# First chunk of the memory keys and values: weights split on POOL into freed token places, turned keys copied earlier

## The reference, cut to what matters

```python
    mix = jnp.concatenate([a, r], axis=-1) @ w_out[l]
    x = x + rms_norm(mix, norm_mix_post[l])

    h = rms_norm(x, norm_xa_pre[l])
    mn = rms_norm(mem, norm_mem[l])
    q = (h @ xa_wq[l]).reshape(B, S, XA_HEADS, XA_HEAD_DIM)
    kv = (mn @ xa_wkv[l]).reshape(B, M, 2, XA_HEADS, XA_HEAD_DIM)
    s = jnp.einsum('bshd,bmhd->bhsm', q, kv[:, :, 0]).astype(jnp.float32) * (XA_HEAD_DIM ** -0.5)
    p = jax.nn.softmax(s, axis=-1).astype(x.dtype)
    xo = jnp.einsum('bhsm,bmhd->bshd', p, kv[:, :, 1]).reshape(B, S, D_MODEL) @ xa_wo[l]
    x = x + rms_norm(xo, norm_xa_post[l])
```

## Time and profile before

| | |
|---|---|
| median of 3 runs | 1456.83 us |
| the profiled execution | 1455.88 us, its span 1453.7 us |
| PE busy | 1413.0 us, 97% of the span |
| POOL busy | 815.1 us, 56% |
| DVE busy | 768.1 us, 53% |
| ACT busy | 610.3 us, 42% |
| granted TensorE clock | 0.999 of 2.4 GHz |
| chain that ended last | PE 82%, DVE 6%, POOL 4%, ACT 3%, DMA 3%, issue 2% |

### The profile page before, as it was taken

The page is one execution under the profiler, slowest core; times in us unless marked ns, Lnnn a source line. Parts: engine busy times, 40 slices in busy tenths (PEclk is TensorE's granted clock), DMA queues, the critical chain, the costliest instruction groups (busy, mean ns, idle before and its releaser), DMA issues.

```text
span 1453.7 us, 19794 instructions
## 1 busy us (share of the span) xinstructions
PE 1413.0 (97%) x7176; PEld 1193.0 (82%) x7176; DVE 768.1 (53%) x1185; ACT 610.3 (42%) x1259; POOL 815.1 (56%) x619
## 2 busy tenths in 40 slices
PE   7999999999999999999999999999999999999998
PEld 7999999766888777888788788888888888867886
DVE  5185048586983776757246843323333333353868
ACT  6111112666642655335446433333333333434454
POOL 1585455001864265530235687777777774699753
PEclk9999999999999999999999999999999999999999
DMA  5452112000025075320245333332333324933353
GB/s 220 149 172 74 50 45 66 0 1 1 9 61 222 34 253 156 94 74 0 85 168 186 104 99 104 109 102 98 106 109 109 107 75 155 366 95 94 99 209 150
DMA packets 119031, 160.29 MB, mean 110 GB/s; under 512 B 9120, under 2 KB 70816, under 8 KB 118944
## 3 DMA queue, kind: packets, MB, share of 16 engines
q1 hardware_dynamic: 115216, 148.93, 31.0%
q10 hardware_dynamic: 3728, 10.24, 2.0%
HBM read 122.17 MB, written 36.96 MB: 109 GB/s over the span
## 4 chain that ended last, share of the span: by engine, by line
PE 82%; DVE 6%; POOL 4%; ACT 3%; DMA 3%; issue 2%; SPq 0%; POOLq 0%; DVEq 0%; ACTq 0%
PE ps L1041 24%; PE ps L1043 24%; PE ps L1042 24%; PE ps L1037 4%; PE ps L1399 2%; DVE z L2541 1%; PE ps L1170 1%; PE ps L1264 1%; DMA raw<-in_xa_wkv_dram 1%; POOL wd L1010 1%; POOL w_lo L914 1%; PE ps L1198 1%; DMA gain_b<-f_rows 1%; PE ps L1242 1%; DVE sm L2416 1%
## 5 line engine op out<-in xcount | busy, mean ns | idle before, releaser
L1041 PE MATMUL ps<-w_hi,t_hi 128*128 128x352 f32 (+1 forms) x768 | 268.0, 349 | 3.7 <-POOL w_lo L930 2.6
L1043 PE MATMUL ps<-w_hi,t_lo 128*128 128x352 f32 (+1 forms) x768 | 265.9, 346 | 0.0
L1042 PE MATMUL ps<-w_lo,t_hi 128*128 128x352 f32 (+1 forms) x768 | 265.3, 345 | 0.0
L1041 PEld LDWEIGHTS ps<-w_hi,t_hi 128*128 128x128 f32 x768 | 144.7, 188 | 15.0 <-POOL w_lo L930 3.4
L1043 PEld LDWEIGHTS ps<-w_hi,t_lo 128*128 128x128 f32 x768 | 144.5, 188 | 11.0
L1042 PEld LDWEIGHTS ps<-w_lo,t_hi 128*128 128x128 f32 x768 | 144.7, 188 | 10.4
L819 POOL TENSOR_TENSOR w_hi<-raw,zero 128x352 fp32r<-128x352 f32 (+1 forms) x68 | 57.9, 852 | 110.7 <-PE ps L1043 110.3
L930 POOL TENSOR_TENSOR w_lo<-raw,w_hi 128x512 fp32r<-128x512 f32 x32 | 41.7, 1315 | 102.1 <-ACT w_hi L1978 101.9
L2864 DVE TENSOR_TENSOR ev<-ps,ev 128x512 f32<-128x512 f32 x21 | 14.5, 691 | 144.2 <-PE ps L1043 144.2
L1696 ACT ACTIVATE z<-ps 128x352 f32 x48 | 22.4, 466 | 162.0 <-PE ps L1043 161.5
L823 POOL TENSOR_TENSOR w_lo<-raw,w_hi 128x352 fp32r<-128x352 f32 (+1 forms) x68 | 77.0, 1133 | 5.3
(11 more groups left out here) (330 smaller groups left out, 3965.7 us busy)
## 6 DMA issues: line engine op xcount, KB each, us to landing
raw_a<-in_ffn_w_gu_dram SPq DMA_DIRECT2D x44, 256.0 KB, 3.1
raw_b<-in_ffn_w_gu_dram SPq DMA_DIRECT2D x44, 256.0 KB, 3.2
f_rows<-fs SPq DMA_DIRECT2D x44, 256.0 KB, 3.7
raw<-in_w_in_dram SPq DMA_DIRECT2D x60, 176.0 KB, 2.3
gain_b<-f_rows SPq DMA_DIRECT2D x39, 256.0 KB, 2.6
tables<-f_rows SPq DMA_DIRECT2D x38, 256.0 KB, 2.7
f_rows<-fa SPq DMA_DIRECT2D x33, 256.0 KB, 3.4
raw<-in_xa_wkv_dram SPq DMA_DIRECT2D x32, 256.0 KB, 3.6
```

The costliest lines, as they stand in the source:

```text
L1041: nc.tensor.matmul(out, a_hi, b_hi, start=start, stop=False, skip_group_check=onto)
L1042: nc.tensor.matmul(out, a_hi, b_lo, start=False, stop=False, skip_group_check=onto)
L1043: return nc.tensor.matmul(out, a_lo, b_hi, start=False, stop=stop, skip_group_check=onto)
```

## The change

The first product's eight units (c = 0) are handled in a new way. POOL waits until tiles 0 to 3 of the last output piece are done. From then on the columns 0 to 511 of `t_hi` and `t_lo` hold token features that nobody reads any more. POOL rounds each unit into `t_hi[:, k, 0:512]` and subtracts into `t_lo[:, k, 0:512]`, and PE reads the weights from there. ACT now rounds units 8 to 31 only, and DVE makes the low parts of units 10, 14, ..., 30 only. On ACT the four roundings ahead of the copy of output tile 7 stay, but they are those of units 8 to 11; the two groups of four behind it are gone. The last change is that the four copies to `kM` now stand ahead of the roundings of units 24 to 27.

The core of the diff:

```diff
@@ -132,7 +132,12 @@
 
 def kv_on_dve(n):
 
-    return n % RING == 2
+    return n >= NK and n % RING == 2
+
+
+def kv_lows(n):
+
+    return n // RING - 1
 
 
 def H2_HI(t):
@@ -677,7 +682,7 @@
                 c, k = divmod(n, NK)
                 dst, src = raw[:, k % RING, :], wkv_v[k, :, c * 512:(c + 1) * 512]
                 if n >= RING and kv_on_dve(n - RING):
-                    sp.wait_ge(kv_low, n // RING)
+                    sp.wait_ge(kv_low, kv_lows(n - RING))
                     sp.dma_start(dst, src).then_inc(w_loaded[k % RING], 16)
                 else:
                     load(U_KV + c * NK, k, dst, src)
@@ -908,13 +913,21 @@
             def mem_low(n):
 
                 k = n % RING
-                pool.wait_ge(mem_rounded, n + 1)
+                pool.wait_ge(mem_rounded, n - NK + 1)
                 if n and kv_on_dve(n - 1):
-                    pool.wait_ge(kv_low, n // RING + 1)
+                    pool.wait_ge(kv_low, kv_lows(n - 1))
                 nc.gpsimd.tensor_tensor(w_lo[:, k, :], raw[:, k, :], w_hi[:, k, :].bitcast(F32),
                                         ALU.subtract).then_inc(w_split, 2 if n and kv_on_dve(n - 1) else 1)
 
-            for n in range(4 * NK):
+            pool.wait_ge(tile_done, TILES["o"] + NT - 1 + 4)
+            for k in range(NK):
+                pool.wait_ge(w_loaded[k % RING], 16 * ((U_KV + k) // RING))
+                nc.gpsimd.tensor_tensor(t_hi[:, k, 0:512], raw[:, k % RING, :], zero[:, 0:1].broadcast_to([P, 512]),
+                                        ALU.add).then_inc(w_rounded, 1)
+                pool.wait_ge(w_rounded, U_KV - RING + k + 1)
+                nc.gpsimd.tensor_tensor(t_lo[:, k, 0:512], raw[:, k % RING, :], t_hi[:, k, 0:512].bitcast(F32),
+                                        ALU.subtract).then_inc(w_split, 1)
+            for n in range(NK, 4 * NK):
                 if not kv_on_dve(n):
                     mem_low(n)
             for n in range(7 * RING):
@@ -1335,13 +1348,17 @@
             def kv_ready(n):
 
                 if kv_on_dve(n):
-                    pe.wait_ge(kv_low, n // RING + 1)
+                    pe.wait_ge(kv_low, kv_lows(n))
                 else:
                     pe.wait_ge(w_split, U_KV + n + 1)
 
+            def first_memory_rows(k, t):
+
+                return m_hi[:, k, t * P:(t + 1) * P], m_lo[:, k, t * P:(t + 1) * P], t_hi[:, k, 0:512], t_lo[:, k, 0:512]
+
             for c in range(4):
                 product(c * NK + U_KV, NM, 512, lambda t: pe.wait_ge(act_ev, kv_seen(c - 2, t)) if c >= 2 else None,
-                        rows_by_weights(m_hi, m_lo, 512), b0=2 * (c % 2), ready=lambda k: kv_ready(c * NK + k),
+                        rows_by_weights(m_hi, m_lo, 512) if c else first_memory_rows, b0=2 * (c % 2), ready=lambda k: kv_ready(c * NK + k),
                         between=turn_keys if c == 2 else lambda: None)
                 if c == 0:
                     pe.wait_ge(act_ev, ACT_EV["h2"])
@@ -1830,10 +1847,10 @@
             def round_units(n):
 
                 nonlocal rounds
-                for _ in range(min(n, 4 * NK - rounds)):
-                    u, slot = U_KV + rounds, (U_KV + rounds) % RING
+                for _ in range(min(n, 3 * NK - rounds)):
+                    u, slot = U_KV + NK + rounds, (U_KV + NK + rounds) % RING
                     act.wait_ge(w_loaded[slot], 16 * (u // RING))
-                    act.wait_ge(w_used, u - RING + 1 if rounds >= RING else u - NK + 1)
+                    act.wait_ge(w_used, u - RING + 1 if rounds >= RING else u - 2 * NK + 1)
                     nc.scalar.activation(w_hi[:, slot, :], raw[:, slot, :], ACT.Copy).then_inc(mem_rounded, 1)
                     rounds += 1
 
@@ -1878,9 +1895,7 @@
             round_units(RING)
             upper_out(7)
             sums(("post", 7), ("pre", 4))
-            round_units(RING)
             sums(("pre", 5))
-            round_units(RING)
             def q_round(n):
 
                 act.wait_ge(w_loaded[n % RING], 16 * ((U_Q + n) // RING))
@@ -1893,6 +1908,7 @@
                         act.wait_ge(turned, TURNED_K + i + 1)
                         nc.scalar.activation(kM[:, 2 * i:2 * i + 2, :], bank(4 + i).rearrange("p (k m) -> p k m", k=2),
                                              ACT.Copy).then_inc(act_ev, 1)
+                    round_units(RING)
                 if c == 3:
                     for n in range(3):
                         q_round(n)
@@ -1915,7 +1931,7 @@
                     sums(("pre", 7))
                     round_units(RING)
                 else:
-                    round_units(NK)
+                    round_units(RING)
             act.wait_ge(added, NT)
             act.dma_start(gain_a[:, :], rows(norm_xa_post)).then_inc(ga_in, 16)
             act.wait_ge(scaled, 2 * NT + NM)
@@ -2603,7 +2619,7 @@
             def kv_unit_low(n):
 
                 k = n % RING
-                dve.wait_ge(mem_rounded, n + 1)
+                dve.wait_ge(mem_rounded, n - NK + 1)
                 nc.vector.tensor_tensor(w_lo[:, k, :], raw[:, k, :], w_hi[:, k, :].bitcast(F32),
                                         ALU.subtract).then_inc(kv_low, 1)
 
@@ -2624,9 +2640,7 @@
             post_rows(4)
             post_rows(5)
             pre_rows(3)
-            kv_unit_low(2)
             post_rows(6)
-            kv_unit_low(6)
             post_rows(7)
             kv_unit_low(10)
             row_lows(0)
```

## The result

In the first comparison the changed kernel took 1451.89 us (median of 6 runs, 1450.14 to 1452.91) beside 1457.66 us for the kernel before (6 runs): a ratio of 0.9959, 95% interval 0.9949 to 0.997. In a second one it took 1452.46 us (7 runs) beside 1458.43 us (22 runs): 0.9966, 0.9953 to 0.9979. (Such a ratio is not the quotient of the two medians; that would be 0.9960 and 0.9959, within both intervals.) It is faster, by 5 to 6 us; 1452.1 was predicted. The profiled execution took 1452.4 us, its span is 1450.5 us. PE is busy for 1413.4 us, before for 1413.0; the change took idle time away, not work.

A forecast was written before the change was run, and what follows sets the result against it. PE, busy 97% of the span, was the bound, so only its waits could give. From the median 1456.83 us, -2.2 (first units to POOL) and -2.46 (keys copied earlier) made -4.7: 1452.1 us, 8-in-10 range 1449.0 to 1456.0.

The forecast's parts named there:

- POOL's 16 instructions: POOL rounds and subtracts the first eight units from 476.5; 19.1 us alone, with DVE turns ending at 504.5.
- Nine meetings at 0.99: Nine DVE instructions with two SBUF operands take turns with POOL's, each adding 0.99 us to the 495.6 end.
- From the split of unit 7 to the rounding of unit 11: Load of unit 11 waits for POOL's split of unit 7; from split to rounding 3.1 us, 504.5 to 507.6.
- First term: First eight units moved to POOL: ACT's rounding of turned token tiles starts at 515.3 instead of 517.49, 2.2 us earlier.
- The chain behind moves as a whole: From token roundings through the load of unit 19 to the keys' turn, same instructions as before, all shifted by 2.2 us.
- Part 2: Keys copied on ACT ahead of the roundings of units 24 to 27: PE's wait of 2.46 us goes.
- cover of 0.5 for unit 28: In the last product unit 28 is ready at 549.9, wanted at 550.4; up to 1 us may come back.
- Turns cost less: Rival: POOL slips between DVE rows, unit 7 done by 501 or earlier; -6.7 us in all, 1450.2 us; chance 0.22.
- Only part 2 pays: Rival: unit 7 split at 506.7 or later, first term 0 to +1.0; 1454.4 to 1455.4 us; chance 0.20.
- Slower: Rival: all 16 POOL instructions lose a turn, unit 7 split at 511.4, ACT holds tile 7's copy; 1459.1 us; chance 0.05.
- break-even: Split of unit 7 on POOL later than 509.2 (504.5 + 4.7) would make the kernel slower.

The follow-up runs named there:

- e4: Changed kernel with POOL's splits starting when output tile 4 is done instead of tile 3: 1455.87 us, ratio 0.9984 to the kernel before.
- e9: Changed kernel with DVE's low parts of units 14 and 22 ahead of its token rows 4 and 6: 1451.26 us, ratio 0.996 to before.
- e1: Kernel before with only the key copies moved ahead of the roundings of units 24 to 27: 1454.0 us, ratio 0.9973 to before.
- e2: Changed kernel with the key copies put back behind the roundings of units 24 to 27: 1454.15 us, ratio 0.9979 to before.
- e3: Changed kernel with ACT's roundings of units 8 to 11 behind the copy of output tile 7 and three sums: 1450.66 us, ratio 0.995 to before.
- e5: Changed kernel with DVE's output rows 3 to 5 and token rows 1 to 3 cut to 8 of 1024 columns: 1449.47 us, ratio 0.9949 to before.
- e6: Changed kernel with the first eight roundings on ACT, POOL only subtracting: 1450.64 us, ratio 0.9952 to before.
- e7: e6 with DVE's low parts of units 14 and 22 ahead of its token rows 4 and 6: 1448.19 us, ratio 0.9938 to before.
- e8: e3 with DVE's low parts of units 14 and 22 ahead of its token rows 4 and 6: 1447.71 us, ratio 0.9936 to before.
- before_again: Kernel before, unchanged, run once more with a profile of its own: 1457.89 us, ratio 1.0 to before.

## Why the prediction was right

- **POOL's 16 instructions.** Nine meetings at 0.99, end at 504.5. Measured: nine long rows, beside the very nine DVE instructions that were counted, end at 504.38. Against the copy of tile 3 it is 27.45 where the sum had 28.0, since a meeting cost 0.92; the whole execution lay 0.44 later there.
- **From the split of unit 7 to the rounding of unit 11.** 3.1 predicted, 3.83 measured (504.38 to 508.21), so this term was 0.7 us too small. Why this load is the longer is not shown; in e4 it took 2.9. The steps behind it took 7.60 (508.21 to 515.81) where the sum had 7.7. The three errors, -0.6, +0.7 and -0.1, cancel; that is luck.
- **First term, 2.2.** Measured 2.12, as the distance from tile 3 to the token roundings (41.00 to 38.88).
- **The chain behind moves as a whole.** From those roundings to the keys' turn: 19.53 before (537.02 less 517.49), 19.69 after (535.50 less 515.81). It does, though the load of unit 19 took 5.07, and e9 shows that this load will not follow an earlier issue.
- **Part 2, 2.46.** The wait is gone; e1 and e2 show it gone alone and back again. From the token roundings to the turn of tiles 4 and 5 it is 30.29 before and 27.81 after, 2.48 less. The cover of 0.5 for unit 28 held: PE had no wait in the last product, which took 12.75 (543.62 to 556.37) against 12.92.
- **The rivals.** "Turns cost less" is wrong: they cost 8.25 us in all. "Only part 2 pays" is wrong: e2 has 2.2 without it. "Slower" has the mechanism right, as e4 shows, and POOL was 5.3 us short of its break-even (27.4 against 32.7 behind tile 3).
- **Whole against stage.** The stage gives 4.8, the medians 5.8 and 6.0, the ratios 4.4 to 7.4 and 3.1 to 6.9. Both intervals hold the stage's 4.8, so the mechanism accounts for the gain within the noise. That 1452.1 lies only 0.2 beside 1451.89 is in part luck: the sum started from 1456.83, and the kernel before took 1457.66 in the comparison. What the prediction did not have, and what may be the rest, is the clock (last section).

## What to carry to other kernels

Work moved to an engine that shares ports is priced by counting its partners in that stretch, one price for each meeting; that count was right here where the length alone was 8 us off. Then ask how much of a delay gets through: behind an in-order engine that holds a copy back for a load, moving the copy ahead (e3) was worth as much as removing all the meetings (e5), because both end at the same next limit, PE's first product. And in a stretch where the DMA engines are full, a load that was issued 2.0 us earlier landed 0.1 earlier (e9).

## What was not expected of the hardware

The granted clock falls behind short idle times of PE, in some executions and not in others. The clearest pair is in the later output stage, which the change does not touch. PE waits there 2.60 us for a low part in every profile. Of after:

```profile
696.42 0.50 PE L1054 MATMUL ps<-w_hi,t_hi 128*128 128x512 f32 x1 [2.60 <-POOL w_lo L943]
```

```profile
696.00:698.00 2.00, 1.57 (x6) 1.29 (x7) 0.00 (x0) 0.58 (x2) 2.00 (x3) 0.94 0.26 89
698.00:700.00 2.00, 2.00 (x6) 1.58 (x5) 0.00 (x0) 0.00 (x0) 2.00 (x2) 0.50 0.52 186
700.00:702.00 2.00, 2.00 (x7) 1.57 (x7) 0.00 (x0) 0.63 (x1) 0.50 (x2) 0.70 0.61 200
```

Of before, the stretch behind the same idle (2.61, ending at 700.76), where nothing fell:

```profile
700.00:702.00 2.00, 1.24 (x5) 1.05 (x6) 0.00 (x0) 0.91 (x2) 2.00 (x3) 1.00 0.15 33
702.00:704.00 2.00, 2.00 (x10) 1.65 (x9) 0.00 (x0) 0.12 (x1) 2.00 (x2) 1.00 0.73 206
```

In the middle 2 us of after 6 matmuls ran, in 702 to 704 of before 10. From the last turn of the stage to the next turn of tokens it is 196.65 us in after (556.37 to 753.02) and 195.04 in before (560.70 to 755.74), so such a fall costs 1.6 us here; over all profiles with it the stretch is 196.5 to 196.8, over those without 195.0 to 195.1. That is why the spans of the two profiled executions differ by 3.2 us and not by the stage's 4.8. Both profiles of after and those of e1, e5, e6, e7 and e9 have it there, both of before and those of e2, e3, e4 and e8 do not, with the same 2.6 us of idle; the one of before_again has it behind the kM wait instead.

For 68 executions of before and 13 of after, the clock is recorded. The mean granted clock of an execution and its time go together:

| mean granted clock | before: runs, mean us | after: runs, mean us |
|---|---|---|
| 0.999 | 18, 1456.07 | 5, 1451.56 |
| 0.998 | 30, 1457.67 | 8, 1452.38 |
| 0.997 | 11, 1458.91 | none |
| 0.996 and 0.995 | 9, 1460.77 | none |
| all | 68, 1457.86 | 13, 1452.07 |

At an equal clock after is ahead by 4.5 and 5.3 us, about what the stage says; over all runs by 5.8, because before more often has a low clock. That fits with one idle time of 2.46 us less at which the clock can fall, and the other kernels count the same way. Before, e2 and e4 have a PE wait of 2.4 to 2.5 us in the stage (e4's is for unit 12), and 28 of their 86 executions are below 0.998 (20 of 68, 2 of 7, 6 of 11). The others have none, and of theirs it is 2 of 60, both of e9. A fall behind that wait itself is seen in one profile only, and what else the executions below 0.998 had is not recorded, so how much of the last microsecond is due to it stays open.
